# A trunk kernel on Trainium2: the first two gate/up pairs taken in five parts with the input

## The reference

```python
def rms_norm(x, w, eps=NORM_EPS):
    y = xf * lax.rsqrt(jnp.mean(xf * xf, axis=-1, keepdims=True) + eps)
    return y * w
def swiglu(x, w_gate, w_up, w_down):
    return (jax.nn.silu(x @ w_gate) * (x @ w_up)) @ w_down

for i in range(DEPTH):                 # 2
    h = h + 0.5 * swiglu(rms_norm(h, norm_ff1[i]), ...)   # D_FF 2816
    h = h + mixer_i(rms_norm(h, norm_mix[i]))             # SSD and RG-LRU, or attention
    h = h + 0.5 * swiglu(rms_norm(h, norm_ff2[i]), ...)
return rms_norm(h, final_norm)
```

## Time and profile before

| | |
|---|---|
| median of 3 runs | 1048.32 us |
| the profiled execution's own time | 1047.69 us |
| its span | 1045.9 us |
| PE busy | 1036.4 us (99%) |
| DVE busy | 803.0 us (77%) |
| ACT busy | 615.6 us (59%) |
| chain that ended last, PE's share | 95% |
| start of pair 2 on PE | 20.42 us |
| period of a pair in the loop after | 5.57 us |

### The profile page before, as it was taken

How to read it: one execution, slowest core, us unless ns; L and a number is a source line. 1 busy time by engine, 2 the same in 40 slices (tenths; PEclk the granted TensorE clock), 3 DMA queues, 4 the chain that set the end, 5 groups by cost and what they waited for, 6 DMA issues and landing times.

```text
span 1045.9 us, 18314 instructions
## 1 busy us (share of the span) xinstructions
PE 1036.4 (99%) x6542; PEld 931.6 (89%) x6542; DVE 803.0 (77%) x1192; ACT 615.6 (59%) x979; POOL 51.0 (5%) x70
## 2 busy tenths in 40 slices
PE   9999999999999999999999999999999999999997
PEld 8888888999999988888888888888998998888886
DVE  7888777699768888887766888776689678887763
ACT  7655554478878775555435555543456766556541
POOL 0200012100000000000111000011100000000021
PEclk9999999999999999999999999999999999999999
DMA  9866766559445666666865666676555456667671
GB/s 264 222 189 194 211 195 178 161 154 277 136 119 154 174 199 191 191 191 180 222 181 161 191 190 191 190 220 174 151 165 168 121 155 196 193 188 207 180 207 40
DMA packets 363298, 190.12 MB, mean 182 GB/s; under 512 B 6080, under 2 KB 360672, under 8 KB 363248
## 3 DMA queue, kind: packets, MB, share of 16 engines
q1 hardware_dynamic: 362848, 188.79, 63.9%
q0 software_dynamic: 256, 0.59, 0.3%
q10 hardware_dynamic: 144, 0.10, 0.1%
HBM read 187.86 MB, written 1.07 MB: 181 GB/s over the span
## 4 chain that ended last, share of the span: by engine, by line
PE 95%; DVE 2%; ACT 1%; SPq 1%; issue 1%; DMA 0%; DVEq 0%; ACTq 0%
PE psum L270 44%; PE psum L279 23%; PE psum L240 7%; PE psum L244 6%; PE psum L241 6%; PE psum L1832 1%; PE psum L255 1%; PE psum L1837 1%; PE psum L258 1%; PE psum L1760 1%; DMA raw<-in_ffn_gate 0%; PE psum L1103 0%; SPq L194 0%; PE psum L1120 0%; DVE xn L376 0%
## 5 line engine op out<-in xcount | busy, mean ns | idle before, releaser
L229 DVE TENSOR_TENSOR wlo<-raw,whi 128x1024 fp32r<-128x1024 f32 (+1 forms) x322 | 415.0, 1307 | 69.5 <-ACT whi L224 68.3
L224 ACT ACTIVATE whi<-raw 128x1024 fp32r<-128x1024 f32 (+1 forms) x322 | 351.9, 1113 | 23.4 <-PE psum L244 19.7
L270 PE MATMUL psum<-xn,whi 128*128 128x512 f32 x1328 | 317.4, 391 | 0.0
L270 PEld LDWEIGHTS psum<-xn,whi 128*128 128x128 f32 x1328 | 244.3, 188 | 47.4
L279 PEld LDWEIGHTS psum<-xn,wlo 128*128 128x128 f32 x1328 | 170.3, 191 | 6.5
L279 PE MATMUL psum<-xn,wlo 128*128 128x256 f32 x1328 | 172.3, 283 | 0.0
L270 PE MATMUL psum<-hid,whi 128*128 128x512 f32 x704 | 166.5, 390 | 0.0
L270 PEld LDWEIGHTS psum<-hid,whi 128*128 128x128 f32 x704 | 129.9, 188 | 25.6
L240 PE MATMUL psum<-xn,whi 128*128 128x256 f32 x416 | 104.5, 289 | 0.0
L241 PE MATMUL psum<-xn,whi 128*128 128x256 f32 x416 | 101.9, 283 | 0.0
L637 ACT ACTIVATE arena<-arena 128x256 f32<-128x256 f32 x88 | 36.8, 418 | 107.4 <-DVE arena L714 107.4
(11 more groups left out here) (252 smaller groups left out, 983.7 us busy)
## 6 DMA issues: line engine op xcount, KB each, us to landing
raw<-in_ffn_down SPq DMA_DIRECT2D x64, 704.0 KB, 4.9
raw<-in_ffn_gate SPq DMA_DIRECT2D x87, 512.0 KB, 3.9
raw<-in_ffn_up SPq DMA_DIRECT2D x87, 512.0 KB, 4.0
raw<-in_hyb_w_in SPq DMA_DIRECT2D x36, 512.0 KB, 4.8
raw<-in_dif_w_qkv SPq DMA_DIRECT2D x24, 512.0 KB, 4.3
raw<-in_hyb_w_out SPq DMA_DIRECT2D x16, 512.0 KB, 4.7
raw<-in_dif_w_o SPq DMA_DIRECT2D x8, 512.0 KB, 3.7
hid<-cs_rows SPq DMA_DIRECT2D x4, 512.0 KB, 6.8
```

The costliest lines, as they stand in the source:

```text
L224: act.activation(whi[:, s, 0:k * P], raw[:, s, 0:k * P], ACT.Copy).then_inc(s_whi, 1)
L229: dve.tensor_tensor(wlo[:, s, 0:k * P], raw[:, s, 0:k * P], whi[:, s, 0:k * P].bitcast(F32), ALU.subtract).then_inc(s_wlo, 1)
L270: mm = pe.matmul(acc, tile_of(whi, s, k)[:, j, :], x[:, k0 + j, :, :], start=opens and j == 0, stop=closes and rest is not None and j == k ...
```

## The change

The begin of the program is rewritten; the loop's body and everything behind the first feed-forward stay. Pairs are counted from 0.

- **Loads.** The five parts are now 1, 1, 2, 2 and 2 tiles, and each holds the rows of both blocks of pairs 0 and 1: one transfer of 256 columns from gate, one from up (1 KB runs where there were 512 B). Pair 2 and pair 3 (blocks 4 to 7) are loaded into free space in `arena` (`load_staged`) with no wait, then pairs 4 and 5 into the ring as soon as the last part is split (`s_wlo` >= 4).
- **PE.** `first_pairs` multiplies pairs 0 and 1 part by part. Pair 2 goes to banks 6 and 7. Then PE waits for two merges, does pair 3 with the token sums between its blocks, pair 4 without a wait, waits for four merges, does pair 5, and the loop runs from pair 6. Of the 13 products of zeros 2 are left.
- **ACT and DVE.** Each part is split in a gate half and an up half; from the second part on both halves wait for both transfers (`s_part[i]` >= 32). Then the orders below.

```diff
-PARTS = ((0, 2), (2, 4), (4, 6), (6, 7), (7, 8))
+PARTS = ((0, 1), (1, 2), (2, 4), (4, 6), (6, 8))
+STAGED = 9216
...
+        def part_hi(act, i, w):
+            if i == 0:
+                act.wait_ge(s_up if w else s_part[0], 16)
+            else:
                 act.wait_ge(s_part[i], 32)
...
+        def staged_hi(act, s):
+            act.wait_ge(s_blk, s + 1)
+            act.wait_ge(s_staged[s], 16)
+            act.activation(whi[:, s, 0:SLOT_IN], staged(s), ACT.Copy).then_inc(s_whi, 1)
...
@@ ffn_sync
+                    for w in range(2):
+                        load_part(sp, i, w, (gate, up)[w])
+                for s in range(RING):
+                    load_staged(sp, s, (gate, up)[s % 2], 2 * P + (s // 2) * P)
+                    if s == 1:
+                        sp.dma_start(con[:, 0:P], a["con"][:, 0:P]).then_inc(s_ones, 16)
+                gate_up(2)
...
@@ ffn_tensor
-                first_pair()
-                zero_products(5)
+                first_pairs()
+                gate_up(p0 + 2, 0, (banks[6], banks[7]))
+                pe.wait_ge(s_gu, 2)
                 for m in range(2):
                     if m:
                         token_sums(pe, n)
-                    multiply_wide(pe, 2 * (p0 + 1) + m, 2 + m, DT, xn, 0, wide(1, m))
-            with pe.Fori(1, FT // 2) as it:
+                    multiply_wide(pe, 2 * (p0 + 3) + m, 2 + m, DT, xn, 0, wide(1, m))
+                gate_up(p0 + 4, 0)
+                pe.wait_ge(s_gu, 4)
+                gate_up(p0 + 5, 1)
+            with pe.Fori(1 if n else 3, FT // 2) as it:
```

More of the change, by code:

```diff
@@ L120, in trunk @@
         s_raw = [sem(f"s_raw{i}") for i in range(RING)]
-        s_part = [sem(f"s_part{i}") for i in range(len(PARTS) - 1)]
+        s_staged = [sem(f"s_staged{i}") for i in range(RING)]
+        s_part = [sem(f"s_part{i}") for i in range(len(PARTS))]
+        s_up = sem("s_up")
         s_dhi = sem("s_dhi")
@@ L304, in wide_parts, with third_parts @@
             return pair[:, :, 0:T], pair[:, :, T:2 * T]
+        def third_parts(g):
+            pair = psum[:, 6:8, :]
+            return pair[:, :, 0:T], pair[:, :, T:2 * T]
         def half(pair, m):
@@ L556, in ffn_tensor, with gate_up @@
             p0, p1, hb = first[n], first[n] + FT, hidden_before(n)
-            def gate_up(p, g):
-                multiply_rows(pe, p * 2, DT, xn, [(2 * g + m, 0, wide(g, m), None, True, True) for m in range(2)])
+            def gate_up(p, g, acc=None):
+                multiply_rows(pe, p * 2, DT, xn, [(2 * g + m, 0, acc[m] if acc else wide(g, m), None, True, True)
+                                                  for m in range(2)])
             def first_gate_up(p, need, before_up):
@@ L581, in first_pair @@
                     if i == 0:
[L582 to L585, removed]
+                        pe.wait_ge(s_xhi, 1)
                         zero_products(2)
[L587 to L599, removed]
+                    if i < LAST:
+                        for w in range(2):
+                            pe.wait_ge(*part_done(i, w, s_phi, s_whi))
+                            rounded((w, w + 2), tiles)
+                        for w in range(2):
+                            pe.wait_ge(*part_done(i, w, s_plo, s_wlo))
+                            rests((w, w + 2), tiles)
+                    else:
+                        pe.wait_ge(s_whi, RING)
+                        rounded((0, 1), tiles)
+                        pe.wait_ge(s_wlo, RING)
+                        rests((0, 1), tiles)
+                        rounded((2, 3), tiles)
+                        rests((2, 3), tiles)
             if n:
@@ L702, in ffn_vector, with merge @@
             p0, hb = first[n], hidden_before(n)
-            def merge(p, q, g, early=False):
+            def merge(p, q, g, early=False, parts=wide_parts):
                 dve.wait_ge(s_blk, p * 2 + 2)
@@ L709, in merge @@
                 dve.wait_ge(s_cor, q + 1)
-                dve.tensor_tensor(gu[:, g, :, :], wide_parts(g)[0], cor[:, g, :, :], ALU.add).then_inc(s_gu, 1)
+                dve.tensor_tensor(gu[:, g, :, :], parts(g)[0], cor[:, g, :, :], ALU.add).then_inc(s_gu, 1)
             def normalize(q, g):
@@ L761, in ffn_vector @@
                 token_scale(dve, n)
-            with dve.Fori(2 if n == 0 else 1, FT // 2) as it:
+            with dve.Fori(3 if n == 0 else 1, FT // 2) as it:
                 for g in range(2):
```

179 lines of the change are left out of this document (103 added, 76 removed).

## The result

| | this | before | ratio, 95% interval |
|---|---|---|---|
| median of 4 runs each | 1053.72 us (1052.66 to 1054.7) | 1048.12 us (1047.25 to 1048.39) | 1.0055 (1.0037 to 1.0072) |
| the profiled execution's own time | 1052.66 us | 1047.69 us | |
| its span | 1050.9 us | 1045.9 us | |

Slower by 5.6 us, 0.5%. The profiled execution is the fastest of the four; the other three took 1.0 to 2.0 us more, a wider spread than that of the kernel before, and it turns out to matter.

What follows compares the result with a forecast made beforehand. PE bounds the kernel, its begin a race against ACT and DVE's chain to the merges. Pair 5 +2.6 us and loop end +0.2 give 1050.5, or 1051.1 from the median; forecast 1050.8, range 1048.6 to 1053.2.

Steps and rivals of the forecast that it cites:

- Pairs 0 and 1 done: Begin of PE: third part's data at 8.6 us, PE starts it at 9.3, both pairs end at 17.6, 2.8 us ahead.
- The rate: Weight loads in the begin: 343 GB/s with 1 KB rows, against 291 for pure 512 B packets.
- The first pause: PE before pair 3, waiting for the second merge: 1.8 us idle, pair 3 starting at 25.0.
- The second pause: PE before pair 5, waiting for the fourth merge: 3.35 us idle.
- the chain: Serial ACT and DVE links from PE's token sums to the end of the fourth merge: 11.95 us, against 8.6 of PE work.
- The tail: End of the gate/up loop: merges lag PE by 0.5 us more, exceeding a slack of 0.25, so +0.2 us.
- The sum: Whole kernel: +2.6 us at pair 5 and +0.2 at the loop's end, +2.8 on 1047.69, hence 1050.5.
- The rival at 0.12: TensorE's clock falls in the new pauses: 1052.2 us if once, costing 1.4, or 1053.6 after both; chance 0.12.
- Chain shorter: Earlier supply or overlapping links leave +1.8 us at 1049.8, no measurable difference; chance 0.11.
- PE's chain decides: Token sums to fourth merge take no longer than PE's 8.6 us: 1047.5, or 1045.8 without first pause; chance 0.07.
- parts starve PE: Parts land as late as 2.9 us each, shifting everything by 0.5 to 1: 1051.5; counted within the 0.70 for computed pauses.
- The rule on descriptor sizes: Fixed 3 cycles per descriptor: 1 KB rows only some 8% faster than 512 B, sum 0.1 us higher.

Runs made afterwards that it cites:

- four parts: Changed kernel with four parts of two tiles instead of five, 12 transfers of 256 KB for the same bytes: 1052.15 us, ratio 1.0046.
- second trace of the unaltered kernel: Changed kernel timed and traced again without any edit, beside the version with its pauses filled: 1054.48 us, ratio 1.0057.
- silu variant: Changed kernel with silu and product of two pairs in a row, then both hidden tiles, on DVE alike: 1053.42 us, ratio 1.0049.
- scale-first variant of five parts: Changed kernel with squares, token sums, root and scale moved earlier, blocks 8 and 9 split between the pairs' steps, its parts kept: 1047.77 us, ratio 0.9997.
- second batch: Changed kernel unedited (1054.48 us) and with unread products in its three PE pauses (1053.02 us), 5 runs each, timed in one batch.
- filled kernel: Changed kernel with matmuls that nothing reads put into its three PE pauses: 1053.02 us, ratio 1.0046.

## Why the prediction was wrong

The direction, the two pauses and what ends them were right. The time, 1053.72 us, lies above the range of 1048.6 to 1053.2. Point by point, in the profiled execution:

- **Pairs 0 and 1 done: predicted 17.6, measured 19.20. This is the step that failed.** I took 8.6 us for the third part's data, on the ground that it ends "the same bytes and requests as before". Taken together they are the same, three requests of 256 KB and six of 128; the order is not. Before, every third request is of 256 KB, the first one too; now the six of 128 KB come first. ACT could round the third part from 10.01, where it began at 8.70 before, and PE began it at 10.69 instead of 9.3. Two things add up: by 8.7 us 1.71 MB had arrived and not 1.93, and when the part was complete, at 10.0, 2.10 MB were there, so more of what stands behind it had come along (0.53 MB beside its 1.57, before 0.36; 0.10 of both are constants). With 256 KB requests for the same bytes the 8.7 came back. The term was +1.4 short at the third part, and +1.6 at the end of the pairs, since parts 3 to 5 took 8.51 us from 10.69 to 19.20 where I had 8.3.
- **The rate.** 343 GB/s for 1 KB rows was right where large requests are queued (351 from 6 to 10 us with four parts) and wrong for the stretch in which it decides (230 and 290).
- **The first pause: predicted 1.8, measured 1.67.** Merge 1 from 25.86 against 24.3, late by the supply's 1.6 alone.
- **The second pause: predicted 3.35, measured 3.12; the chain: 11.95, measured 12.08.** Every link within 0.1. The token sums stand 2.91 behind the start of pair 3, where I had 2.77, since the first matmuls after a pause are further apart. Pair 5: predicted 39.7, measured 41.58, of which 1.6 is the supply, 0.3 the two small ones.
- **The tail: predicted +0.2, measured 0.5** from pair 5 to the end of the span (4.46 to 5.0 late), 0.3 of it at the end of the gate/up loop. The second trace of the unaltered kernel speaks for the reason I gave, merges that lag PE: there the low clock held PE back for 2.67 us while ACT and DVE went on, so the lag was gone, and PE is as late at the narrow products after the loop (145.35, 7.22 late) as it was in the loop (7.24 late).
- **The sum** for the profiled execution: 1050.5 predicted, 1052.66 measured: 1.9 up to pair 5 and 0.3 behind it. This alone would have been inside the range; the median stands 1.06 us above the profiled execution, where I had allowed 0.3, and that took it out.
- **The clock.** The rival at 0.12 was not an alternative to the computed case but an addition to it. Traces show it in the unaltered kernel after 3.12 us, costing 2.67 up to the next pair, where I had 1.4; in the silu variant after 2.44 us, costing some 1.6; and in the scale-first variant of five parts after 2.10. The first trace of the changed kernel does not show it. In the second batch the untraced runs' mean clock shows it, and the filled kernel brought the median down by 1.5 us and the spread from 1.5 to 0.9. For the 1.0 to 2.0 us of the three untraced runs of the result it is likely but not shown. The Trainium skill, "TensorE: Matmul & The Clock Gate", section on the HAM clock gate, warned of such idling; the runs agree that it happens, and show that the same pause may or may not bring it.
- **The other rivals.** Chain shorter and PE's chain decides: no. The case that parts starve PE was the right mechanism at the wrong place. I put it at the late parts, +0.5 to 1, and it came at the third, +1.6; the late ones came in time (ACT waited 0.26 and 0.33 us for them, PE not at all).
- **The rule on descriptor sizes** (the Trainium skill, "DMA: Bandwidth & Descriptors", section "Why small descriptors are slow (HBM only)") that I weighed against the trace was worth 0.1 us either way; what decided was the size and order of whole requests at the start, which I did not question.

## What to carry to other kernels

A start that is bound by the first megabytes, as this one, is not helped by cutting it finer to begin sooner: check what rate small requests reach before you count on the rate of a full queue. Work that is brought forward gains nothing if the wait that follows is fed by a serial chain that starts at a late point of the same engine's program; move the chain's first link before anything else, as the version with the scale first does. And a pause on TensorE should be priced twice, once as itself and once with the clock behind it, as an addition with a chance and not as another case.

## What was not expected of the hardware

- The first requests' size: 128 KB ones brought 230 GB/s from 2 to 6 us and 290 from 6 to 10, 256 KB ones 303 and 351, with the same 1 KB rows. In the kernel before, with 512 B rows of the weights, the small sizes brought 0.83 MB by 6 us instead of 1.03. What holds the small ones back was not tried. A later issue is not it: the changed kernel issues the ninth request 0.25 us before the kernel before does (4.58 against 4.83) and has the data 1.3 us after it.
- The clock after a pause differs from execution to execution of one program: 1.00 and 0.66 granted over the 8.4 us after the same 3.12 us. The traces have it falling after pauses of 2.10, 2.44 and 3.12 us, and not falling after 1.96, nor after 3.12 in two other executions.
- With the lower level granted until 47 us, the 16 wide matmuls from 41.59 on took 6.60 us against 3.92; most of them start 0.43 us apart and not 0.23.
